# Order of the work in the down-projection stage of a decoder trunk: which product slots stand where, and in which slot the side engines do their parts

## The reference, cut to what matters

```
def swiglu(h, w_gate, w_up, w_down):
    return (jax.nn.silu(h @ w_gate) * (h @ w_up)) @ w_down

f = swiglu(rmsnorm(x, pre), w_gate, w_up, w_down)     # w_down: 2816 x 1024
x = x + 0.5 * rmsnorm(f, post)
```

## Time and profile before

| | us |
|---|---|
| time, median of 3 runs | 2115.83 |
| lowest, highest | 2113.25, 2116.8 |
| profiled execution, device time | 2117.45 |
| its span in the trace | 2115.6 |
| TensorE busy | 2085.8 (99%) |
| VectorE busy | 1257.3 (59%) |
| ScalarE busy | 864.1 (41%) |
| mean granted TensorE clock | 0.997 |

### The profile page before, as it was taken

One profiled execution on the slowest core, in us unless ns is written; L12 is line 12 of the kernel. 1 busy time (PEld: TensorE's weight loads), 2 busy tenths in 40 slices (PEclk: granted clock), 3 DMA queues, 4 the chain that ended last, 5 costly groups with the idle time before them and its releaser, 6 DMA issues.

```text
span 2115.6 us, 26156 instructions
## 1 busy us (share of the span) xinstructions
PE 2085.8 (99%) x10362; PEld 1747.6 (83%) x10362; DVE 1257.3 (59%) x1819; ACT 864.1 (41%) x1255; POOL 78.0 (4%) x79
## 2 busy tenths in 40 slices
PE   9999999999999999999999999999999999999998
PEld 8888877888888888988887888888787779888877
DVE  6445577576666644644557755456785646445576
ACT  5222265444555543422236532224554544222263
POOL 0000000000000000000000000000014100000000
PEclk9999999999999999999999999999999999999999
DMA  7566585222111214566677565667634124566684
GB/s 261 209 225 222 201 319 161 81 95 63 60 61 60 71 50 140 189 231 217 208 251 264 164 233 197 227 220 273 231 116 126 54 70 151 208 227 220 203 323 135
DMA packets 144412, 371.29 MB, mean 175 GB/s; under 512 B 10353, under 2 KB 10993, under 8 KB 144290
## 3 DMA queue, kind: packets, MB, share of 16 engines
q1 hardware_dynamic: 83440, 229.14, 34.1%
q10 hardware_dynamic: 60850, 140.47, 17.4%
HBM read 297.22 MB, written 71.30 MB: 174 GB/s over the span
## 4 chain that ended last, share of the span: by engine, by line
PE 94%; DVE 3%; issue 2%; ACT 1%; POOL 0%; ACTq 0%; DVEq 0%; POOLq 0%
PE ps L1166 18%; PE ps L1168 18%; PE ps L1167 18%; PE ps L1174 10%; PE ps L1176 9%; PE ps L1175 9%; PE ps L1479 1%; PE ps L1193 1%; DVE w_lo L1813 1%; PE ps L1698 1%; PE ps L1727 1%; ACT w_hi L587 1%; PE ps L1547 1%; PE ps L1702 1%; PE ps L1403 1%
## 5 line engine op out<-in xcount | busy, mean ns | idle before, releaser
L1166 PE MATMUL ps<-h_hi,w_hi 128*128 128x512 f32 (+1 forms) x1832 | 679.5, 371 | 0.2
L1168 PE MATMUL ps<-h_hi,w_lo 128*128 128x512 f32 (+1 forms) x1832 | 674.0, 368 | 0.0
L1167 PE MATMUL ps<-h_lo,w_hi 128*128 128x512 f32 (+1 forms) x1832 | 673.7, 368 | 0.0
L587 ACT ACTIVATE w_hi<-raw 128x1024 fp32r<-128x1024 f32 x432 | 452.8, 1056 | 507.5 <-PE ps L1168 339.0
L1813 DVE TENSOR_TENSOR w_lo<-raw,w_hi 128x1024 fp32r<-128x1024 f32 x417 | 503.0, 1221 | 139.0 <-ACT w_hi L587 138.1
L1166 PEld LDWEIGHTS ps<-h_hi,w_hi 128*128 128x128 f32 x1832 | 345.4, 189 | 58.2 <-issue 1.8
L1168 PEld LDWEIGHTS ps<-h_hi,w_lo 128*128 128x128 f32 x1832 | 345.3, 188 | 57.6
L1167 PEld LDWEIGHTS ps<-h_lo,w_hi 128*128 128x128 f32 x1832 | 345.6, 189 | 56.4 <-issue 0.2
L1813 DVE TENSOR_TENSOR extra<-a_rows,ps 128x512 f32<-128x512 f32 x88 | 60.5, 688 | 403.7 <-PE ps L1168 380.5
L1174 PE MATMUL ps<-w_hi,a_split 128*128 128x512 f32 x616 | 242.9, 394 | 13.0 <-DVE update L1813 9.0
L1176 PE MATMUL ps<-w_hi,a_split 128*128 128x512 f32 x616 | 241.5, 392 | 0.0
(11 more groups left out here) (241 smaller groups left out, 2231.3 us busy)
## 6 DMA issues: line engine op xcount, KB each, us to landing
raw<-in_w_gate_up SPq DMA_DIRECT2D x176, 512.0 KB, 4.6
a_rows<-in_w_down ACTq DMA_DIRECT2D x44, 1024.0 KB, 9.9
sums<-a_rows ACTq DMA_DIRECT2D x44, 1024.0 KB, 7.9
raw<-sums SPq DMA_DIRECT2D x80, 512.0 KB, 5.2
raw<-in_w_down SPq DMA_DIRECT2D x60, 512.0 KB, 4.3
spilled<-extra ACTq DMA_DIRECT2D x44, 512.0 KB, 4.9
normed<-spilled ACTq DMA_DIRECT2D x44, 512.0 KB, 6.4
raw<-in_w_vg SPq DMA_DIRECT2D x16, 512.0 KB, 3.6
```

Source lines behind the costliest of these rows:

```text
L587: return nc.scalar.activation(to, source, ACT.Copy, scale=scale)
L1166: nc.tensor.matmul(to, w_h, hi, start=first, stop=False)
L1167: nc.tensor.matmul(to, w_h, lo, start=False, stop=False)
L1168: return nc.tensor.matmul(to, w_l, hi, start=False, stop=last)
```

## The change

- Phase A: groups 0 to 3 as before (M6, M5, M1); the last two groups are ordered by product: M1 twice, M6 twice, M5 twice. M1 ends with slot 13 (before 15), M6 with 15 (16), M5 with 17 as before. The half slots are 13, 15 and 17 (before 15, 16 and 17).
- M3: one slot ahead of M4 (before two), so M4 ends with slot 30 (before 31). M3's end, slot 35, and M2's place stay.
- The blocks of the second kind are split at steps 3, 4, 6, 8, 9, 11, 13, 14, 16, 18, 20 (before 3, 5, 7, 8, 10, 12, 14, 16, 17, 19, 21); their reloads go five steps ahead, as before. What the copy waits for is written out for the new order.
- `mean_f` of chunk 0 stands ahead of `scale_late`; `mean_x` of chunk 0 stands a step sooner, ahead of that step's weight split; ScalarE's squares of chunk 1 of x stand a step later.

```diff
-    order = []
-    for m in range(GROUPS):
-        order += [(name, m) for name in (("M1", "M6", "M5") if m == GROUPS - 1 else ("M6", "M5", "M1"))]
-    order += [("M7", m) for m in range(GROUPS)] + [("M3", m) for m in range(2)] + [("M4", m) for m in range(GROUPS)]
-    return order + [("M3", m) for m in range(2, GROUPS)] + [("M2", m) for m in range(GROUPS)]
+    order = [(name, m) for m in range(GROUPS - 2) for name in ("M6", "M5", "M1")]
+    order += [(name, m) for name in ("M1", "M6", "M5") for m in (GROUPS - 2, GROUPS - 1)]
+    order += [("M7", m) for m in range(GROUPS)] + [("M3", 0)] + [("M4", m) for m in range(GROUPS)]
+    return order + [("M3", m) for m in range(1, GROUPS)] + [("M2", m) for m in range(GROUPS)]
...
-REFINED_AFTER = [3 + (9 * j + 2) // 5 for j in range(PAIRS)]
+REFINED_AFTER = [3 + 17 * j // 10 for j in range(PAIRS)]
...
                             act.wait_ge(first_lo, PAIRS * f + PAIRS)
-                            act.wait_ge(slot_done, at + 3 * (j // 2) + 3)
+                            act.wait_ge(slot_done, at + max(DOWN_AT[name, j // 2] for name in ("M1", "M5", "M6")) + 1)
...
                     if k == C21_AFTER + 1 and s + 1 < N_SUB:
                         square_x(s + 1, 0)
+                    if k == C21_AFTER + 2 and s + 1 < N_SUB:
                         square_x(s + 1, 1)
...
                     if k == C21_AFTER:
+                        mean_f(s + 1, 0)
                         scale_late(s + 1, 0)
                         scale_late(s + 1, 1)
-                        mean_f(s + 1, 0)
                         mean_f(s + 1, 1)
                         add_update(s + 1, 0)
                     if k == C21_AFTER + 1:
                         add_update(s + 1, 1)
+                        if s + 1 < N_SUB:
+                            mean_x(s + 1, 0)
                     if k == C21_AFTER + 2 and s + 1 < N_SUB:
-                        mean_x(s + 1, 0)
                         mean_x(s + 1, 1)
                         norm_x(s + 1, 0)
```

## The result

| | before, us | changed, us |
|---|---|---|
| median (four runs each) | 2115.51 | 2092.1 |
| lowest, highest | 2113.25, 2116.8 | 2090.81, 2093.72 |
| profiled execution, its span | 2117.45, 2115.6 | 2093.72, 2091.9 |

The ratio is 0.9894, with a 95% interval from 0.9882 to 0.9907: faster by 1.1%. Forecast were 2091.0 in a range from 2086 to 2103.

What follows compares the result with a forecast made beforehand. TensorE, busy 99% of the span, was taken as the bound, with four waits in the down stages. 14.4 - 0.8 + 4.8 + 5.2 + 3.0 - 1.8 = 24.8 us off 2117.45 gave 2092.65, as median 2091.0; range 2086 to 2103.

Steps and rivals of the forecast that it cites:

- first wait and low clock: TensorE at M7's start (slot 18), waiting for U2, then slow clock; 14.4 us lost, 0.8 expected to remain.
- second wait: TensorE at slot 23, M7's last, idle 0.98 in all four stages; block 10 a step sooner gains 4.8 us.
- third wait: Transposes of chunk 0 behind M2's first slot, three stages; M3's slot moved behind M4 gains 5.2 us.
- fourth wait: Transposes of chunk 2 in the next sub-layer, held by late C11 adds; all 3.0 us expected gained.
- M4's new wait: M4's second columns wait for C22 and U3 adds with one M3 slot as cover; 1.8 us lost over four stages.
- for the forecast speaks that three of four stages had the loads in time: Argument that U2's thin margin before M7 holds in most stages, against the 17% rival of U2 coming late.
- E1: Two blocks ScalarE copies after M1's last slot, in the chain to U2 ahead of M7; with w_hi 2.04 us.
- the margin of 0.48 us: Before M7: chain from M1's end to TensorE takes 7.68 us, covered by 8.16 us of slots 14 to 17.
- The first rival: U2 still late at M7 in most stages through loads; 5.7 us more, 2097, or 2103 with low clock; 17%.
- arrives there relative to TensorE at least 0.95 earlier: VectorE reaches chunk 2's C11 add sooner by at least 0.95 us; 1.17 is needed in the worst stage.
- transposes still waiting: Named sign of a wrong forecast: transposes still wait, where none for normed was expected; no size given.
- Starved reloads: Slower case: moved reloads starve the first phase, w_lo over 7.8 us later; up to 2128 us; 5%.

Runs made afterwards that it cites:

- the five executions with this order: Profiled executions of the changed kernel and four follow-up kernels sharing its order up to M7; lost at M7: 2.64, 0.34, 1.95, 0.24 and 0.90 us.
- the phase-A experiment: Changed kernel with the old order of phase A (M1's last part at slot 15), all else as changed; 2102.88 us, ratio 0.994.
- block 10's step: Changed kernel with block 10 split at step 21 again instead of 20; 2095.51 us, ratio 0.9912.
- the experiment with the old means: Changed kernel with the old order of means and squares, M3's slot and all else as changed; 2097.0 us, ratio 0.9918.
- The late-split kernel: Changed kernel with the mixer's third weight-slot split, behind the first down stage, put behind chunk 2's squares and norm; 2090.65 us, ratio 0.9888.
- The two-slot kernel: Changed kernel with two M3 slots ahead of M4, as before the change; 2090.83 us, ratio 0.9884.

## Why the prediction was right, and where it was not

The gain was 23.7 us in the profiled executions, where 24.8 were worked out. By its steps (losses against the pitch of 0.227 us per matmul):

| step | predicted gain | measured |
|---|---|---|
| first wait and low clock | 13.6 | 11.8 |
| second wait | 4.8 | 4.8 |
| third wait | 5.2 | 5.2 |
| fourth wait | 3.0 | 1.9 |
| M4's new wait | -1.8 | -1.65 |
| transposes no longer behind a wait | not counted | 1.4 |
| sum | 24.8 | 23.45 |

The total came out closer than its terms deserve. The fourth wait went by an edit for which nothing was counted, and without that edit the time is 2097.0, outside the 2088 to 2094 that was given 60%. And what was left at M7 and at chunk 2 of the first stage is offset by half by the transposes, which nobody counted. That the number is within 1.1 us is in part luck.

- **First wait: right mechanism, left-over mis-sized.** 0.8 us were taken, all in the second stage; the profiled execution left 1.25, 0.79 and 0.60 in stages 2 to 4, 2.64 together. The chain is as worked out. In the first stage U2 starts at 299.41, 43.53 us behind 255.88, and TensorE passes M7's start without a wait. In the second the timeline of ScalarE and VectorE has:

```profile
1124.98 1.06 ACT L586 ACTIVATE w_hi<-raw 128x1024 fp32r<-128x1024 f32 x1 [1.58 <-DMA raw<-sums]
...
1127.22 1.22 DVE L1813 TENSOR_TENSOR a_split<-normed,a_split 128x1024 fp32r<-128x1024 f32 x1
1128.36 1.22 DVE L1813 TENSOR_TENSOR w_lo<-raw,w_hi 128x1024 fp32r<-128x1024 f32 x1
1129.49 1.22 DVE L1813 TENSOR_TENSOR a_split<-normed,a_split 128x1024 fp32r<-128x1024 f32 x1
1130.63 1.28 DVE L1813 TENSOR_TENSOR update<-update,ps 128x512 f32<-128x512 f32 x2
```

  The split waits 1.58 for M7's sum row, and the chain of four behind it carries that to U2, 45.23 behind the stage's start. In stages 3 and 4 the same split waits 0.85 and 0.73, and the next one 0.53 and 0.47 more. The step that failed is "for the forecast speaks that three of four stages had the loads in time". In the kernel before, the splits of the last 15 us ahead of M7 wait for no load in those three stages; in the change the split behind E1 does in two of them, and the margin of 0.48 us does not cover it. Nor did the loads land earlier, as was hoped. ScalarE's waits for sum rows in the whole span, before and in the change:

```profile
ACT w_hi L587 <- DMA raw<-sums: 8.0, 9, 2.1
```

```profile
ACT w_hi L586 <- DMA raw<-sums: 16.4, 20, 1.6
```

  The first rival had the right place, and was too dear: 5.7 us more where 1.8 came. The size itself was no bad guess: over the five executions with this order the loss is 1.2 us on average, and the 2.64 above is the largest of them, in the changed kernel's slowest run.
- **No low clock.** Every stage stands at 1.00, and no wait at M7 above 1.02 us is left. Up to TensorE's last matmul, in the profiled executions of all ten kernels, the low clock stands only behind idles of 1.94 us and more at M7, and the phase-A experiment brings it back with the wait, in two stages of four. So it needs that wait here; what decides in which stage it comes is open.
- **Second wait: right**, and shown apart by block 10's step.
- **Third wait: right**, and the experiment with the old means shows that M3's slot alone does it.
- **Fourth wait: the step failed in part.** It said that C11 "arrives there relative to TensorE at least 0.95 earlier" by the slot. The old-means kernel shows it 0.45 later; what removed the wait in stages 2 and 3 was the part for which "I count nothing" was written at the third wait (all but 0.23, which the slot adds to it). In stage 1 it stayed whole, which is one of the signs of being wrong that the prediction named ("transposes still waiting"). The cause was not in it; it is on ScalarE's and VectorE's timeline:

```profile
362.44 1.06 ACT L586 ACTIVATE w_hi<-raw 128x1024 fp32r<-128x1024 f32 x1 [2.69 <-PE ps L1176]
...
363.54 1.22 DVE L1813 TENSOR_TENSOR w_lo<-raw,w_hi 128x1024 fp32r<-128x1024 f32 x1 [1.46 <-ACT w_hi L586]
```

  The split has to wait until M2's slot 40 has released its weight buffer, and the squares and `norm_x` of chunk 2 stand behind it. In stage 2 the same split reuses the buffer of slot 38, and there it starts at 1190.50, 2.9 us ahead of the last matmul instead of 0.2. In the kernel before it started at 369.02, the same 0.2 ahead of 369.21. TensorE's own progress sets this wait, so no gain elsewhere could shorten it, and it was 1.12 before and after. The late-split kernel removes it.
- **M4's new wait: right** to 0.04 in each stage: 0.17 and 0.18 idle with the slower next step, 0.41 lost against 0.45. The two-slot kernel takes it away. The 1.65 us bought next to nothing, though, since the third wait would have gone by the means and squares alone.
- **The transposes** were not counted. Behind a wait eight of them take 1.32 us, without one 1.03, five times 0.28:

```profile
348.84 1.03 PE L1193 MATMUL ps<-ident,normed 128*128 128x128 f32 x8
```

- **The other rivals.** Starved reloads: no `w_lo` wait in the first twelve slots, and 2092.1. Short waits that bring the clock down: the changed kernel has seven from 0.17 to 1.02 in these places and none is followed by the low level.

**What stays open**: why the same order leaves 2.64 us at M7 in one execution and 0.24 in another. ScalarE waits for the same sum row of the second stage 1.58 us in the changed kernel and 0.40 with two M3 slots; which transfer it collides with was not isolated.

## What to carry to other kernels

When a product is moved ahead, count how many splits now stand between two side jobs that are tied to different slots: the gain at the first can be paid back at the second, as 0.69 - 1.14 here. A wait for a buffer that the bound engine itself releases is not shortened by making the helper faster; only what stands behind it can be moved ahead. A margin smaller than the spread of a load's landing (0.48 us here, against waits of 0.4 to 2.3 for one row) is to be priced in every stage, not only in the one that showed a late load: in the five executions M7 was late in 8 of 20 stages. Taking one piece out of the chain, block 7, covered it. And one traced execution is one draw: compare several before a difference of 1 or 2 us is put down to an edit.

## What the runs showed of the hardware that was not expected

- The low clock is no sure consequence of an idle of about 2 us. Of the eight idles of 1.94 us and more at M7 (1.94, 3.21, 1.94, 1.94 before; 1.95, 1.95, 2.32, 1.94 with phase A back) five were followed by 4 us with a mean granted clock of 0.57 to 0.65, three were not, the one of 2.32 among these. A price of 1.6 us belongs to it times a chance, not in full. None of the shorter idles, up to 1.71 (the old-means kernel, second stage), was followed by it:

```profile
1132.20:1136.20 4.00, 3.92 (x17) 3.28 (x18) 4.00 (x5) 2.24 (x3) 0.00 (x0) 1.00 0.74 259
```

- A wait costs more than its idle. At a 512-column matmul 0.17 idle was 0.41 lost, and at eight transposes a further 0.28 to 0.29 went into the work itself.
